# Samples' value rows projected in four column groups, and the output gate of tokens 256 to 519 projected in the second pass

## The reference

```python
xn = rmsnorm(h, norm1_g)
qa, ka, va, qb, kb, vb, rb, ab, gza, gzb = split(xn @ w_in)   # 3 x 512, 2 x 256, 2 x 512, 16, 2 x 1024
qa, ka = rmsnorm(qa, qa_norm_g), rmsnorm(ka, ka_norm_g)       # 8 heads of 64
ya = stick_breaking_attention(qa, (past_k, ka), (past_v, va)) # samples: 4096 cached tokens, in 32 pages each
log_a = log_sigmoid(ab @ w_alpha + b_alpha) / 16
ob, s_new = gated_linear_attention(qb, kb, vb, log_a, s0)     # 4 heads, keys of 64, values of 128
yb = rmsnorm(ob, ob_norm_g) * silu(rb)
h = h + (sigmoid(gza + b0) * (ya @ w_up_a) + sigmoid(gzb + b1) * (yb @ w_up_b)) @ w_o
h = h + peer(rmsnorm(h, norm2_g))   # 8 heads x top 16 of 16384 experts per token, each one row of u and one of v
h = h + (p @ w_ple) * sigmoid(rmsnorm(h, norm3_g) @ w_ple_gate)
```

## Time and profile before

| | |
|---|---|
| median of 3 runs | 2098.89 us (2097.85 to 2099.18) |
| span of the profiled execution | 2094.6 us |
| what lies around the span, against the median | 4.3 us |
| busy: PE, DVE, ACT, POOL | 1597.0, 1366.9, 657.2, 788.0 us |
| DMA | 769.21 MB, mean 367 GB/s |
| the chain that ended last | 39% DMA, 35% PE, 11% DVE |

### The profile page before, as it was taken

The page is one execution under the profiler, slowest core; times in us unless marked ns, Lnnn a source line. Parts: engine busy times, 40 slices in busy tenths (PEclk is TensorE's granted clock), DMA queues, the critical chain, the costliest instruction groups (busy, mean ns, idle before and its releaser), DMA issues.

```text
span 2094.6 us, 23943 instructions
## 1 busy us (share of the span) xinstructions
PE 1597.0 (76%) x8018; PEld 735.3 (35%) x8018; DVE 1366.9 (65%) x2675; ACT 657.2 (31%) x1837; POOL 788.0 (38%) x881
## 2 busy tenths in 40 slices
PE   8999979999997777776788577666467658466686
PEld 6637634477254323333322133333012112112122
DVE  1688789876047776666555557778567787545543
ACT  3123144521022234444322323323233423223332
POOL 1232233322353443333334443444244444344541
PEclk9999989999998979989899799899768779798888
DMA  4677889998898999999999999999999999999993
GB/s 168 217 259 256 301 311 327 324 348 288 313 364 323 418 415 417 418 409 420 402 415 419 395 420 419 420 394 420 417 395 404 410 403 422 392 421 421 421 421 161
DMA packets 157019, 769.21 MB, mean 367 GB/s; under 512 B 26456, under 2 KB 26936, under 8 KB 89312
## 3 DMA queue, kind: packets, MB, share of 16 engines
q0 software_dynamic: 103072, 637.59, 75.7%
q1 hardware_dynamic: 53824, 130.10, 17.3%
HBM read 759.41 MB, written 5.58 MB: 365 GB/s over the span
## 4 chain that ended last, share of the span: by engine, by line
DMA 39%; PE 35%; DVE 11%; issue 5%; POOL 5%; ACT 4%; SPq 0%; POOLq 0%; DVEq 0%; ACTq 0%
DMA arena<-experts_in,arena 37%; PE bank L2177 9%; PE bank L1725 6%; DVE arena L193 5%; POOL arena L761 5%; DVE arena L1666 4%; PE bank L1783 3%; PE bank L1806 3%; PE bank L2032 3%; PE bank L2089 2%; PE bank L2155 2%; PE bank L2060 1%; ACT arena L1197 1%; DVE arena L1262 1%; PE bank L2044 1%
## 5 line engine op out<-in xcount | busy, mean ns | idle before, releaser
L2177 PE MATMUL bank<-arena 64*64 64x512 f32 x4096 | 633.3, 748 | 433.2 <-ACT arena L1197 423.5
L1666 DVE CUSTOM_DVE_ANT_0 arena<-arena 128x1024 f32<-128x1024 f32 x520 | 631.1, 1226 | 476.0 <-DMA arena<-experts_in,arena 464.7
L761 POOL DMA_INDIRECT arena<-experts_in,arena x520 | 597.0, 1148 | 829.8 <-PE bank L2177 703.3
L2177 PEld LDWEIGHTS bank<-arena 64*64 64x64 f32 x4096 | 158.3, 159 | 856.0 <-ACT arena L1197 612.4
L1186 ACT ACTIVATE arena<-arena 128x2 f32<-128x2 f32 x260 | 53.3, 205 | 893.2 <-DVE arena L1666 865.7
L721 POOL DMA_DIRECT2D arena<-cache_k_in x256 | 137.8, 538 | 358.0 <-DVE arena L1262 288.4
L1262 DVE TENSOR_TENSOR arena<-arena 128x1024 f32<-128x1024 f32 x128 | 156.4, 1224 | 23.2 <-DMA arena<-scratch_q 11.0
L1197 ACT ACTIVATE arena<-arena 128x64 f32<-128x64 f32 (+1 forms) x520 | 153.3, 343 | 8.4
L1250 DVE TENSOR_REDUCE arena<-arena 128x16 f32<-128x1024 f32 x128 | 155.2, 1215 | 0.0
L2032 PE MATMUL bank<-arena 128*128 128x256 f32 (+1 forms) x512 | 126.3, 404 | 10.9 <-DVE arena L193 6.7
L193 ACT ACTIVATE arena<-bank 128x260 f32<-128x260 f32 (+7 forms) x116 | 48.0, 427 | 267.3 <-PE bank L1725 107.4
(11 more groups left out here) (101 smaller groups left out, 1354.3 us busy)
## 6 DMA issues: line engine op xcount, KB each, us to landing
arena<-cache_k_in POOLq DMA_DIRECT2D x256, 256.0 KB, 5.1
arena<-w_stream_in SPq DMA_DIRECT2D x120, 512.0 KB
arena<-cache_v_in SPq DMA_DIRECT2D x160, 256.0 KB, 5.4
arena<-cache_v_in POOLq DMA_DIRECT2D x96, 256.0 KB, 5.5
arena<-experts_in,arena POOLq DMA_INDIRECT x520
arena<-xT_in SPq DMA_DIRECT2D x4, 520.0 KB, 6.6
arena<-scratch_q SPq DMA_DIRECT2D x1, 2048.0 KB
arena<-x_rows_in SPq DMA_DIRECT2D x2, 1024.0 KB
```

Of the source, the lines that this page charges most:

```text
L761: pool.indirect_dma_start(gring[:, s, :], None, A["experts"], bass.IndirectOffsetOnAxis(ap=rows, axis=0)).then_inc(g_landed[s], 16)
L1666: last = V.tensor_tensor_reduce(gring[:, s, 0:D], gring[:, s, 0:D], x_rows, 1.0, 0.0, ALU.mult, ALU.add, dot[:, s:s + 1])
L2177: last = mm(bank[2 * r + c2][out, :], diag[rows, s], gring[rows, s, cols], start=start, stop=True, skip_group_check=True)
```

## The change

First, the samples' rows of the value projections. Before, each feature tile had a matmul of 8 stationary columns. Now the samples' columns of `xn` are copied, padded to 32 with zeros (`xs_pad`), and four feature tiles at a time are multiplied in four column groups of PE, each into its own 32 partitions of a bank. ACT copies that bank to SBUF (`vs_sums`), a matmul with a 0/1 matrix of 8 columns adds the four partial sums (`fold_samples`), and ACT takes the result to `vab` (`take_sample_rows`). The weight tiles of two steps are now released by the matmuls of one burst.

Second, the output gate `rb`. In the front it is projected for tokens 0 to 255 alone, in four `late` pieces. For tokens 256 to 519 the four weight tiles are loaded a second time and projected in the gather's steps 7 to 10 (`rb_tiles`), ACT takes a sigmoid one step later, and DVE multiplies the sigmoid with the bank and with `srb` another step later (`rb_rows`). `ob_norm` therefore leaves the gate out for those tokens.

```diff
+RB_AT = 7
@@ slots of the weight ring
+            if rb_use(0) <= n < rb_use(RB_USES):
+                return gate_ready, 16 + n - rb_use(0) + 1
@@ ScalarE
+            def take_sample_rows(n):
+                act.wait_ge(vs_ready, n + 1)
+                o = (512, 0)[n]
+                c.also(A_, vab[0:NB, NT, o:o + 512], bank[6 + n][0:NB, :], ACT.Copy, signal=vs_taken)
...
-            for n in range(10, 16):
-                late(n)
+            late(10)
+            late(11)
...
+            def rb_sigmoid(m):
+                a, b = PASS_COLS[1]
+                act.wait_ge(gate_ready, 16 + m + 1)
+                if m >= 2:
+                    act.wait_ge(rb_done, m - 1)
+                c.also(A_, rb_tmp[:, m % 2, 0:b - a], bank[4 + m % 2][:, 0:b - a], ACT.Sigmoid, signal=gate_taken)
@@ VectorE
+            dve.wait_ge(front_set, 5)
+            c.then(V.tensor_copy, xs_pad[:, :, 0:NB], xn[:, :, SEQ:T], signal=xn_ready)
...
+            def rb_rows(m):
+                a, b = PASS_COLS[1]
+                dve.wait_ge(gate_taken, 16 + m + 1)
+                silu = rb_tmp[:, m % 2, 0:b - a]
+                c.also(V.tensor_tensor, silu, silu, bank[4 + m % 2][:, 0:b - a], ALU.mult)
+                c.then(V.tensor_tensor, srb[:, m, a:b], srb[:, m, a:b], silu, ALU.mult, signal=rb_done)
@@ TensorE
+            def fold_samples(n):
+                i = VB_ITEM + 5 * n + 4
+                pe.wait_ge(proj_taken, i + 1)
...
+                mm(bank[6 + n][0:NB, :], cst("own_head"), vs_sums[n], start=True, stop=True).then_inc(vs_ready, 1)
...
-                    for t in range(5):
+                    for t in range(NT):
...
+                    if q % 2 == 1:
+                        out = item(made_items[0] + NT) if q == 1 else bank[(made_items[0] + NT) % 6]
+                        for k in range(2 * q - 2, 2 * q + 2):
+                            rows = slice(32 * (k % 4), 32 * (k % 4) + 32)
+                            wk = weights(FRONT.index(s0 + k // 2)).rearrange("p (k c) -> p k c", k=2)[:, k % 2]
+                            last = mm(out[rows], xs_pad[:, k], wk, start=(k < 4), stop=(k >= 4), skip_group_check=True)
+                            if k in (2 * q - 1, 3):
+                                last.then_inc(kstep, 1)
...
-                project_half(S_KA + n // 2 if n < 8 else S_RB + (n - 8) // 2, n % 2)
+                if n < 8:
+                    project_half(S_KA + n // 2, n % 2)
+                else:
+                    project_half(S_RB + n - 8, 0, PASS_COLS[0])
...
+            def rb_tiles(m):
+                a, b = PASS_COLS[1]
+                w = weights(rb_use(m)).rearrange("p (k c) -> p k c", k=KD)
+                if m < 2:
+                    pe.wait_ge(pq_taken, 15 + m)
+                else:
+                    pe.wait_ge(rb_done, m - 1)
+                for k in range(KD):
+                    last = mm(bank[4 + m % 2][:, 0:b - a], w[:, k], xn[:, k, a:b], start=(k == 0), stop=(k == KD - 1))
                 last.then_inc(gate_ready, 1)
```

More of the change, by code:

```diff
@@ L802, in take @@
                     o = 0 if kind == "va" else 512
-                    R = ROWS[j]
-                    c.also(A_, vab[0:R, j, o:o + 512], item_bank(i)[0:R, :], ACT.Copy, signal=proj_taken)
-                else:
-                    c.also(A_, srb[:, j, a:b], src, ACT.Silu, signal=proj_taken)
+                    out = vab[:, j, o:o + 512] if j < NT else vs_sums[kind == "va"]
+                    c.also(A_, out, item_bank(i), ACT.Copy, signal=proj_taken)
+                else:
+                    a, b = PASS_COLS[0]
+                    c.also(A_, srb[:, j, a:b], item_bank(i)[:, 0:b - a], ACT.Silu, signal=proj_taken)
+            def take_sample_rows(n):
+                act.wait_ge(vs_ready, n + 1)
+                o = (512, 0)[n]
+                c.also(A_, vab[0:NB, NT, o:o + 512], bank[6 + n][0:NB, :], ACT.Copy, signal=vs_taken)
             def norm_buffers(j):
@@ L856, in _ @@
             c.then(A_, la_tmp, la_tmp, ACT.Exp, scale=-1.0)
[L857 removed]
+            c.then(A_, la_tmp, la_tmp, ACT.Ln, bias=1.0, signal=gla_e)
             for t in range(2):
@@ L866, in _ @@
             c.also(A_, sample_decay, la[:, :, SEQ:T], ACT.Exp, scale=1.0 / TAU, signal=gla_e)
-            for i in range(VB_ITEM + 2, LATE_ITEM):
+            for i in range(VB_ITEM + 2, VB_ITEM + 5):
+                take(i)
+            take_sample_rows(0)
+            for i in range(VB_ITEM + 5, LATE_ITEM):
                 take(i)
@@ L1389, in ob_norm @@
                 dve.wait_ge(ob_std, 2 * (h + 1))
-                c.also(V.scalar_tensor_tensor, out=srb[:, h], in0=ob[:, h], scalar=vecs[:, V_OG:V_OG + 1], in1=srb[:, h],
+                (a, b), (a2, b2) = PASS_COLS
+                c.also(V.scalar_tensor_tensor, out=srb[:, h, a:b], in0=ob[:, h, a:b], scalar=vecs[:, V_OG:V_OG + 1], in1=srb[:, h, a:b],
                        op0=ALU.mult, op1=ALU.mult)
-                c.then(V.tensor_tensor, srb[:, h], srb[:, h], ob_tmp[:, h % 3], ALU.mult, signal=yb_ready)
+                c.also(V.scalar_tensor_tensor, out=srb[:, h, a2:b2], in0=ob[:, h, a2:b2], scalar=vecs[:, V_OG:V_OG + 1],
+                       in1=ob_tmp[:, h % 3, a2:b2], op0=ALU.mult, op1=ALU.mult)
+                c.then(V.tensor_tensor, srb[:, h, a:b], srb[:, h, a:b], ob_tmp[:, h % 3, a:b], ALU.mult, signal=yb_ready)
             for h in range(GH):
@@ L1715, in _, with project_half @@
             made_items = [0]
-            def project_half(s, half):
+            def project_half(s, half, cols=None):
                 w = weights(FRONT.index(s)).rearrange("p (k c) -> p k c", k=KD)
-                a, b = HALVES[half]
-                out = item(made_items[0])[:, 0:HALF]
+                a, b = cols or HALVES[half]
+                out = item(made_items[0])[:, 0:b - a]
                 made_items[0] += 1
@@ L1924, in _ @@
             key_mean(7, 1)
-            late(8)
-            sample_values(0)
-            late(9)
-            sample_values(1)
-            for b in range(2, NB):
-                late(8 + b)
+            for b in range(0, NB, 2):
+                late(8 + b // 2)
                 sample_values(b)
-                if b < NB - 1:
-                    v_half(0, b + 1)
+                if b >= 2:
+                    v_half(0, b // 2 + 2)
+                sample_values(b + 1)
+            v_halves(0, 6, 8)
             pe.wait_ge(ss_ready, 1)
```

86 lines of the change are left out of this document (58 added, 28 removed).

## The result

The changed kernel takes **2086.3 us** (median of 4 runs, 2084.72 to 2087.02) beside 2098.37 us of the kernel before on the same chip (2097.42 to 2099.18): ratio 0.9941, 95% interval 0.9922 to 0.9960. A second series on another chip gave 2084.03 beside 2096.57 us, ratio 0.9945 (0.9927 to 0.9964); one execution of the kernel before took 3203 us there and is left out of that ratio. The forecast was 2085.9.

The account below looks back on a forecast made before the run. The gather was taken as bound by DMA bytes, the stages before it by compute (PE, DVE). Front -18 plus gather +5 gave -13 us: span 2081.6, time 2085.9 us, range 2079 to 2094.

Parts of the forecast that it names:

- Value projections, 8.6 us: PE's value projections: sample rows in column groups plus two folds save 8.6 us, from 14.2 - 3.8 - 1.8.
- Rival 2: Value projections: column groups don't overlap, PE 1.8 us later instead of 8.6 earlier; 2093.9 us, chance 5%.
- DVE's first wait, 4.4 us: DVE's 4.51 us wait for ScalarE's exponentials at 117.9 us practically goes, as they come 4.4 us earlier.
- 7.1 us ahead at the samples: DVE reaches its sample stage, at 209 us, 7.1 us earlier; bounds 4.4 and 8.6.
- Sample stage: DVE's eight samples start 3.63 us apart instead of 5.74, saving 12.8 us, less 1.9 for the last value pages.
- Front, -18 us: All stages ahead of the gather together: 18 us earlier, later stages shifting unchanged; bounds 11 and 19.5 us.
- rival 1: Sample stage: transfers at their limit eat part of the front's gain; 2092.4 us, chance 17%.
- Weight ring, 0: Value weight tiles: 0 to 1.9 us of stall, twice, covered by PE's 4.2 us slack; without cover up to 4 us.
- Gather, +5.0 us: Gather: four weight tiles loaded again, 2.097 MB at 419 GB/s, cost 5.0 us with compute alongside; bounds 0 and 28.
- Rival 3: Gather: ring of eight slots loses 7 us in each of four steps, 28 us; slower at 2108.9 us, chance 8%.
- rival 4: Gather: the reloaded bytes find gaps and cost nothing, leaving -18 us; 2080.9 us, chance 7%.
- 4.3 us "around the span": Whole run: profiled span of 2094.6 us lies 4.3 below the median 2098.89; this difference was taken to stay.

Follow-up runs that it names:

- groups_only: Against the kernel before: only the value projections' column groups added, output gate left wholly in the front; 2089.98 us, ratio 0.9963.
- second profile: Profiled execution of the changed kernel, unedited, run again in another series beside the kernel before; median 2084.03 us, ratio 0.9945, span 2082.4 us.
- gate_only: Against the kernel before: only the output gate's second half moved to the gather, samples' value rows left as before; 2089.02 us, ratio 0.9952.

## Why the prediction was right

**Value projections, 8.6 us: right.** Four bursts at 0.99 us are 4.0 us, forecast 3.8; two folds 2 x 0.96 = 1.9, forecast 1.8. The 128 full-width records take 55.9 us from start to start (13.85 and 13.96 for the first two 32), 0.437 each, so of the 70.96 us before the 32 narrow ones had 15.1, not the 14.2 that an equal share for every record gives: saved are 15.1 - 4.0 - 1.9 = 9.2 us. That the transposes came 9.8 us earlier is this and the second fold, which now lies behind them, less some tenths. The groups overlap: a burst is 0.1 us over a pure quarter of its eight records (8 x 0.4435 / 4 = 0.89 us), which is all the room there is for what a change of the mode costs. The page TensorEngine Tiling (Array Packing) of the Trainium skill says that changing the tiling mode drains TensorE (Tiling Modes, Key Properties). The trace leaves such a drain 0.1 us a burst. Rival 2 is out.

**DVE's first wait, 4.4 us: right.** It is gone with the groups and is there, at 4.29 us, without them.

**7.1 us ahead at the samples: right in size, and first misread.** The first profile shows 5.2, and I took the term for mis-sized by the round trip over ScalarE and PE. The second shows 7.5 and `groups_only` 7.4. From the transposes to the first sample it is 63.4 us in the first profile and 61.7 in `groups_only`: 1.6 us of the difference are the clock's, in one execution.

**Sample stage: right.** 3.67 us apart for 3.63 forecast. Own heads wait for the value pages as foretold, with DVE let go at 235.25 in the second profile ("about 235"), 17.9 us early for 18. In the first profile a page came late (2.84 us of PE's wait).

**Front, -18 us: a little too much.** 16.8 in the second profile, 14.9 in the first. The step that failed is "After 253 us nothing is removed: DVE's 48 us and PE's 122 us shift as they are". From own heads to PE's entry into the heads it is 50.6 us in the first profile and 49.2 in the second, where it was 48.2. A key page is waited for 3.60 and 2.21 us there instead of 0.65; over the five profiles of this code it is 1.8 to 3.9. `gate_only` has that wait, `groups_only` has not, so it comes with the shortened sample stage. The DMA engines are at a share of 1.02 at 385 GB/s there, where it was 0.97 at 362, but the page that is late lands 6.16 us after its issue, where the one waited for before took 7.95. It is late because POOL issues it late, by 2.6 us in the first profile. That transfers at their limit hold it, rival 1 in small, is therefore not shown, and why POOL is late is open. In the sample stage itself DVE waits for no key page. From the entry into the heads to the first gather it is 338.4 to 345.2 us over all thirteen profiles (before 340.5, after 339.1 and 340.6). `groups_only` lost 4.8 us there and the changed kernel nothing. Which landings make this is open.

**Weight ring, 0: right.** No weight tile is waited for in the value projections.

**Gather, +5.0 us: right.** 5.6 and 4.6 us in the two profiles, 5.9 as a mean over all. The bytes cost it and the work does not: with the work cut it was 1459.5 us, with the bytes cut 1450.7 and 1452.3. Rival 3 is out by that, and rival 4 (the bytes find gaps) by the gap between the two groups of profiles.

**The sum.** -16.8 + 4.6 = -12.2 us by the second profile, 12.1 and 12.5 us by the two pairs of medians, -13 forecast. That the time of 2085.9 us was met to 0.4 us is luck: the front was off by 1.2 to 3.1 us in the two profiles, and single executions of one kernel lie 2 us and more apart. The 4.3 us "around the span" are not one thing either. In every run that has both numbers it is 1.6 to 2.0 us, so the profiled execution of the kernel before was some 2.4 us faster than the median. The forecast goes by a difference, so this does not touch it, but all shifts above are counted from that one execution.

## What to carry to other kernels

Here work that was moved from a compute-bound stage into one that is bound by bytes cost its bytes and nothing else, because the ring there held through it: look at the DMA share of a window that has such work already. A stage that is shortened asks for its successor's loads sooner. For a load that comes late then, read both when it was issued and how long it took: here the DMA share of the stage had risen, and yet the page was late mostly by its issue. Before a mis-sized term is explained, compare a second profile at the same place: here 1 to 5 us of a milestone were an accident of the execution.

## What was not expected of the hardware

The granted clock halved in a single execution behind a wait of 1.89 us (2.08 us for what takes 1.16), while waits of 1.84 and 1.73 us at the same place in two other profiles left it at full. Behind DVE's wait at the heads it differs too. The first two records there take 2.08 us in some profiles and 1.12 or 1.13 in others (287.76 us above; 284.44 in the second profile). Waits of 3.30 to 5.89 us went before 2.07 or 2.08 us in six profiles and one of 3.61 before 1.80; but 2.43 us went before 2.08, and 2.60 and 2.81 before 1.12 and 1.13.

The 1457 us from the first gather to the end lie within 3 us over nine profiles on different chips. The 340 us ahead of them scatter by 4.3 in the five profiles whose code is the same there (339.1 to 343.4), and by 6.8 over all thirteen.

POOL's 3.15 us between the first and second page of one set of eight stand in every profile at the same set (before from 263.61 us, there waited for by nobody), and what they are the profile does not name.
